# A feed-forward down projection by Strassen's seven products in eight of its eleven weight tiles, in a float32 kernel

## What is computed

```python
def swiglu(h, w_gate, w_up, w_down):
    return (jax.nn.silu(h @ w_gate) * (h @ w_up)) @ w_down
...
x = x + 0.5 * swiglu(rmsnorm(x, norm_g[layer, 0]), ffn_w_gate[layer, 0], ffn_w_up[layer, 0], ffn_w_down[layer, 0])
```

## Time and profile before

| | |
|---|---|
| median of 3 runs | 2626.75 us (2625.58 to 2626.8) |
| the profiled execution | 2626.32 us, of which the span is 2624.5 |
| granted TensorE clock, mean of the span | 0.999 |
| busy: TensorE, VectorE, ScalarE, GpSimd | 99%, 69%, 57%, 10% |
| HBM read over the span | 179 GB/s |

### The profile page before, as it was taken

How to read it: one execution, slowest core, us unless ns; L and a number is a source line. 1 busy time by engine, 2 the same in 40 slices (tenths; PEclk the granted TensorE clock), 3 DMA queues, 4 the chain that set the end, 5 groups by cost and what they waited for, 6 DMA issues and landing times.

```text
span 2624.5 us, 35122 instructions
## 1 busy us (share of the span) xinstructions
PE 2605.2 (99%) x14596; PEld 2241.7 (85%) x14596; DVE 1822.5 (69%) x2239; ACT 1493.7 (57%) x1974; POOL 258.6 (10%) x246
## 2 busy tenths in 40 slices
PE   8999999999999999999999999999999999999999
PEld 7888778888888878888889998888888899988888
DVE  6667766666667766666668887666666688876765
ACT  5456765445446655445457767454454577674543
POOL 0003210000004110000003123100000021231000
PEclk9999999999999999999999999999999999999999
DMA  7654445555555445555556464555555564645553
GB/s 239 198 189 161 161 158 182 191 193 182 189 175 181 152 161 188 189 184 193 192 166 187 138 211 159 179 190 190 179 193 193 167 189 135 210 159 183 186 193 128
DMA packets 342747, 471.84 MB, mean 180 GB/s; under 512 B 18810, under 2 KB 259516, under 8 KB 342588
## 3 DMA queue, kind: packets, MB, share of 16 engines
q1 hardware_dynamic: 342588, 469.61, 54.9%
HBM read 468.46 MB, written 1.11 MB: 179 GB/s over the span
## 4 chain that ended last, share of the span: by engine, by line
PE 94%; DVE 2%; ACT 2%; DMA 0%; issue 0%; SPq 0%; POOL 0%; DVEq 0%; ACTq 0%
PE PS L100 91%; PE PS L103 3%; DVE WL L109 1%; ACT ME L106 1%; ACT WH L106 1%; DMA ST<-in_ffn_w_gate 0%; DVE RL L117 0%; DVE XB L117 0%; DVE ME L109 0%; SPq L142 0%; ACT RH L106 0%; DVE SB L114 0%; POOL XB L109 0%; DVE SB L120 0%; DVE EA L109 0%
## 5 line engine op out<-in xcount | busy, mean ns | idle before, releaser
L109 DVE TENSOR_TENSOR WL<-ST,WH 128x2048 fp32r<-128x2048 f32 (+3 forms) x442 | 1005.5, 2275 | 352.8 <-ACT WH L106 351.7
L100 PE MATMUL PS<-XHL,WH 128*128 128x512 f32 (+1 forms) x4096 | 1123.6, 362 | 3.8 <-DVE GS L109 2.7
L106 ACT ACTIVATE WH<-ST 128x2048 fp32r<-128x2048 f32 (+3 forms) x442 | 830.7, 1880 | 144.4 <-PE PS L100 136.9
L100 PEld LDWEIGHTS PS<-XHL,WL 128*128 128x128 f32 x3456 | 652.8, 189 | 124.7
L100 PE MATMUL PS<-XHL,WL 128*128 128x256 f32 x3456 | 735.3, 279 | 0.0
L100 PEld LDWEIGHTS PS<-XHL,WH 128*128 128x128 f32 x4096 | 634.4, 190 | 12.9 <-DVE GS L109 2.8
L100 PE MATMUL PS<-WH,XHL 128*128 128x512 f32 (+3 forms) x1472 | 460.9, 387 | 0.0
L100 PE MATMUL PS<-WH,RH 128*128 128x512 f32 (+1 forms) x1056 | 410.3, 389 | 3.4 <-DVE RL L109 1.9
L100 PE MATMUL PS<-WL,RH 128*128 128x512 f32 (+1 forms) x1056 | 407.9, 386 | 0.0
L100 PE MATMUL PS<-WH,RL 128*128 128x512 f32 (+1 forms) x1056 | 407.6, 386 | 0.0
L100 PEld LDWEIGHTS PS<-WH,XHL 128*128 128x128 f32 x1472 | 273.7, 188 | 58.4 <-issue 7.3
(11 more groups left out here) (247 smaller groups left out, 1955.8 us busy)
## 6 DMA issues: line engine op xcount, KB each, us to landing
ST<-in_ffn_w SPq DMA_DIRECT2D x132, 1024.0 KB, 5.0
ST<-in_w_in SPq DMA_DIRECT2D x106, 1024.0 KB, 5.2
ST<-in_ffn_w_down SPq DMA_DIRECT2D x44, 1024.0 KB, 4.9
ST<-in_ffn_w_gate SPq DMA_DIRECT2D x43, 1024.0 KB, 5.3
ST<-in_ffn_w_up SPq DMA_DIRECT2D x43, 1024.0 KB, 5.3
ST<-in_w_ssd_out SPq DMA_DIRECT2D x16, 1024.0 KB, 5.0
ST<-in_w_branch SPq DMA_DIRECT2D x8, 1024.0 KB, 5.0
ST<-in_w_out SPq DMA_DIRECT2D x8, 1024.0 KB, 5.0
```

The source lines that it names most:

```text
L100: return self.eng.matmul(o, l, r, start=start, stop=stop) if self.eng else Said()
L106: return self.eng.activation(o, v, f, **kw) if self.eng else Said()
L109: return self.eng.tensor_tensor(o, a, b, op) if self.eng else Said()
```

## The change

Seen by blocks, a down tile is a 2 x 2 product: the hidden tile has four 128-column blocks (two k-halves by two halves of the 256 rows of X), the weight tile four 512-column blocks. Strassen's form (in Winograd's variant) has seven block products instead of eight, with sums of blocks on both sides.

- The phase's order becomes all 22 gate and up tiles (steps 0 to 21), then the eleven down tiles (steps 22 to 32). All eleven hidden tiles are kept.
- Down tiles 0, 5 and 10 (`PLAIN`) keep eight products. The other eight (`SUMMED`) take seven, four of them on sums of weight blocks (kind "t", in `TS`, split into `TH` and `TL`, rings of three) and three on the blocks themselves (kind "q", in `WH` and `WL`, of which the first 512 columns are no longer split for these tiles).
- `tile_sums` makes the weight sums on GpSimd, in float32 from `ST`, in three operations of 1024, 512 and 512 columns. `pair_sums` makes four sums of 128 columns of the hidden tile, and `scale_up` multiplies the up half by RBC, both on GpSimd. The reciprocal norm is now in the hidden tile, and no longer in the residual.
- `load_tile` waits for the sums of the tile that leaves its slot, besides its low part.
- All eight banks add up over the phase, one per kind of product (`MBANK`). Tiles 9 and 10 are run together, bank by bank. X is then put together from the eight banks and UM, by `add_um` (two SBUF inputs) and `add_product` (PSUM and X), one of the `add_um` on GpSimd.
- The transposes of X's first half follow the last bank's matmuls. The split of the next phase's first tile is made by GpSimd (`weights_lo` at the end of `pool_ffn`).
- The rope tables move to steps 16 to 18 of the first phase, and the transposes of the constants' gains from the first mixer's steps 0 and 1 to step 18 of the first phase.

```diff
-FFN = [("g", 0), ("u", 0), ("g", 1), ("u", 1)]
-for _i in range(2, NP):
-    FFN += [("g", _i), ("u", _i), ("d", _i - 2)]
-FFN += [("d", NP - 2), ("d", NP - 1)]
+FFN = [(_w, _i) for _i in range(NP) for _w in ("g", "u")] + [("d", _i) for _i in range(NP)]
 UP_AT = {i: FFN.index(("u", i)) for i in range(NP)}
 GATE_AT = {i: FFN.index(("g", i)) for i in range(NP)}
+DOWN = 2 * NP
...
+HIDDEN_AT = [max(UP_AT[i] + 1, 3) for i in range(NP - 1)] + [UP_AT[NP - 1] + 2]
...
+PLAIN = (0, 5, 10)
+SUMMED = [_i for _i in range(NP) if _i not in PLAIN]
+SEVEN = (("m1", 0, "q", 1), ("m2", 2, "q", 3), ("m3", 6, "q", 2), ("m6", 5, "t", 2), ("m5", 3, "t", 0), ("m7", 4, "t", 1),
+         ("m4", 1, "t", 3))
+EIGHT = (("m2", 1, "q", 1), ("m2", 3, "q", 3), ("m3", 1, "q", 0), ("m3", 3, "q", 2), ("c22", 0, "q", 0), ("c22", 2, "q", 2),
+         ("m4", 0, "q", 1), ("m4", 2, "q", 3))
+MBANK = {"m1": 0, "m6": 6, "m5": 4, "m7": 5, "m2": 1, "m3": 3, "c22": 7, "m4": 2}
...
+    def tensor_product(e, p, i, name, a, kind, c, begun, last=False):
+        tile, b = T0[p] + DOWN + i, MBANK[name]
+        c = slice(c * 512, (c + 1) * 512)
+        if kind == "q":
+            e.wait_ge(*at("lo", tile))
+            wh, wl = WH[:, tile % NR, c], WL[:, tile % NR, c]
+        else:
+            n = SUMMED.index(i) % 3
+            wh, wl = TH[n][:, c], TL[n][:, c]
+            e.wait_ge(*at("tl", p, i))
+        e.wait_ge(*at("hl", p, i))
+        first = b not in begun
+        if first:
+            clear(b)
+            begun.add(b)
+        fh, fl = HH[i][:, of(a)], HL[i][:, of(a)]
+        e.matmul(PS[:, b, :], fh, wh, first, False)
+        e.matmul(PS[:, b, :], fh, wl, False, False)
...
+                if i < NP - 2:
+                    for name, a, kind, c in EIGHT if i in PLAIN else SEVEN:
+                        m = tensor_product(e, p, i, name, a, kind, c, begun)
+                    m.then_inc(*e.done("tile", tile))
+                elif i == NP - 2:
+                    for group in MBANK:
+                        own = [(j, r) for j in (i, i + 1) for r in (EIGHT if j in PLAIN else SEVEN) if r[0] == group]
+                        for j, (name, a, kind, c) in own:
+                            m = tensor_product(e, p, j, name, a, kind, c, begun, (j, (name, a, kind, c)) == own[-1])
+                        m.then_inc(*e.done(group, p))
+                        if group == "m3":
+                            e.also("tile", tile)
+                    e.also("tile", tile + 1)
+                    freed.update({0: ("um", p), 1: ("x", p, 1, 1), 2: ("x", p, 0, 1), 3: ("x", p, 1, 0), 4: ("x5", p),
+                                  5: ("x7", p), 6: ("um", p), 7: ("x", p, 0, 0)})
+                    if p + 1 < len(phases):
+                        turn_x(e, p + 1, "", 0)
...
+        a, n = 512 if i in SUMS else 0, plan[i][0] * plan[i][1]
...
+    def sums_hi(e, p, i):
+        n = SUMMED.index(i)
+        e.wait_ge(*at("ts", p, i))
+        if n in (1, 2):
+            e.wait_ge(*at("tile", T0[p] + UP_AT[NP - 1]))
+        elif n > 2:
+            e.wait_ge(*at("tile", T0[p] + DOWN + SUMMED[n - 3]))
+        e.activation(TH[n % 3], TS[n % 3], ACT.Copy).then_inc(*e.done("th", p, i))
...
+            elif s == len(FFN) - 2:
+                e.wait_ge(*at("m1", p))
+                e.wait_ge(*at("tile", t0 + DOWN + NP - 3))
+                e.activation(UM, PS[:, MBANK["m1"], :], ACT.Copy, scale=0.5).then_inc(*e.done("uv", p))
+                weights_hi(e, t0 + s + 2)
...
+    def sums_lo(e, p, i):
+        e.wait_ge(*at("th", p, i))
+        n = SUMMED.index(i) % 3
+        e.tensor_tensor(TL[n], TS[n], TH[n].bitcast(F32), ALU.subtract).then_inc(*e.done("tl", p, i))
+    def hidden_lo(e, p, i):
+        e.wait_ge(*at("hh", p, i))
+        e.tensor_tensor(HL[i], H8[i][:, 128:128 + HN[i]], HH[i].bitcast(F32), ALU.subtract).then_inc(*e.done("hl", p, i))
+    def add_product(e, p, name, t, n, f, *done):
+        e.wait_ge(*at(name, p))
+        x = X[:, t, half(n)]
+        e.stt(x, PS[:, MBANK[name], :], f, x, ALU.mult, ALU.add).then_inc(*e.done(*done))
+    def add_um(e, p, t, n):
+        x = X[:, t, half(n)]
+        e.tensor_tensor(x, x, UM, ALU.add).then_inc(*e.done("xu", p, t, n))
...
+            if s == DOWN + NP - 3:
+                sums_lo(e, p, NP - 2)
+            if s < len(FFN) - 2:
+                weights_lo(e, t0 + s + 2)
+            if s + 1 - DOWN in SUMMED and s < DOWN + NP - 3:
+                sums_lo(e, p, s + 1 - DOWN)
...
+            if s == len(FFN) - 1:
+                e.wait_ge(*at("uv", p))
+                add_um(e, p, 1, 1)
+                e.wait_ge(*at("m6", p))
+                e.wait_ge(*e.last())
+                e.stt(UM, PS[:, MBANK["m6"], :], 0.5, UM, ALU.mult, ALU.add).then_inc(*e.done("um", p))
+                e.wait_ge(*e.last())
+                add_um(e, p, 1, 0)
+                add_um(e, p, 0, 0)
+                e.wait_ge(*at("xu", p, 1, 0))
+                add_product(e, p, "m5", 1, 0, -0.5, "x51", p)
+                e.wait_ge(*at("xu", p, 0, 0))
+                add_product(e, p, "m5", 0, 0, -0.5, "x5", p)
+                e.wait_ge(*e.last())
+                add_product(e, p, "m7", 0, 0, 0.5, "x70", p)
+                e.wait_ge(*at("xu", p, 1, 1))
+                add_product(e, p, "m2", 1, 1, 0.5, "x", p, 1, 1)
+                e.wait_ge(*at("x51", p))
+                add_product(e, p, "m3", 1, 0, 0.5, "x", p, 1, 0)
+                e.wait_ge(*at("xu", p, 0, 1))
+                add_product(e, p, "m7", 0, 1, 0.5, "x7", p)
+                e.wait_ge(*at("x70", p))
+                add_product(e, p, "c22", 0, 0, 0.5, "x", p, 0, 0)
+                if p + 1 < len(phases):
+                    split_x_lo(e, p + 1, "", 0)
+                e.wait_ge(*at("x7", p))
+                add_product(e, p, "m4", 0, 1, 0.5, "x", p, 0, 1)
+                weights_lo(e, t0 + s + 2)
...
+    def pool_ffn(e, p):
+        t0 = T0[p]
+        for s in range(len(FFN)):
+            for n, i in enumerate(SUMMED):
+                if s == DOWN - 3 + i + (n > 2):
+                    tile_sums(e, p, i)
+            for i in range(NP):
+                if s == UP_AT[i] + 1:
+                    scale_up(e, p, i)
+                if s == HIDDEN_AT[i] + 1 and i in SUMMED:
+                    pair_sums(e, p, i)
+        e.wait_ge(*at("um", p))
+        add_um(e, p, 0, 1)
+        weights_lo(e, t0 + len(FFN))
...
+    def scale_up(e, p, i):
+        h = HQ[i].rearrange("p (k t) -> p k t", k=2)
+        e.wait_ge(*at("us", p, i))
+        e.wait_ge(*at("rbc", p))
+        e.tensor_tensor(h, h, RBC[:, :].unsqueeze(1).to_broadcast([128, 2, T]), ALU.mult).then_inc(*e.done("un", p, i))
+    def pair_sums(e, p, i):
+        a21, a11, a22, a12, s1, s3, s2, s4 = (H8[i][:, of(j)] for j in range(8))
+        e.wait_ge(*at("m", p, i))
+        e.tensor_tensor(s1, a21, a22, ALU.add).then_inc(*e.done("s1", p, i))
+        e.tensor_tensor(s3, a11, a21, ALU.subtract).then_inc(*e.done())
+        e.wait_ge(*at("s1", p, i))
+        e.tensor_tensor(s2, s1, a11, ALU.subtract).then_inc(*e.done("s2", p, i))
+        e.wait_ge(*at("s2", p, i))
+        e.tensor_tensor(s4, a12, s2, ALU.subtract).then_inc(*e.done("s4", p, i))
+    def tile_sums(e, p, i):
+        tile, n = T0[p] + DOWN + i, SUMMED.index(i)
+        q = [ST[:, tile % NS, j * 512:(j + 1) * 512] for j in range(4)]
+        t1, t2, t4 = (TS[n % 3][:, j * 512:(j + 1) * 512] for j in (0, 2, 3))
+        e.wait_ge(*landed[tile])
+        if n > 2:
+            e.wait_ge(*at("tile", T0[p] + DOWN + SUMMED[n - 3]))
+        elif n == 2:
+            e.wait_ge(*at("m", p, NP - 2))
+        elif p == 0:
+            e.wait_ge(*at("gt", 3))
+            e.wait_ge(*at("cos", 1))
+            e.wait_ge(*at("rope_tables", 1))
+        e.tensor_tensor(TS[n % 3][:, 0:1024].rearrange("p (a c) -> p a c", a=2),
+                        ST[:, tile % NS, 512:1536].rearrange("p (a c) -> p a c", a=2),
+                        q[0].unsqueeze(1).to_broadcast([128, 2, 512]), ALU.subtract).then_inc(*e.done("t1", p, i))
+        e.wait_ge(*at("t1", p, i))
+        e.tensor_tensor(t2, q[2], t1, ALU.add).then_inc(*e.done("t2", p, i))
+        e.wait_ge(*at("t2", p, i))
+        e.tensor_tensor(t4, q[3], t2, ALU.subtract).then_inc(*e.done("ts", p, i))
...
+            if i - NS in SUMS:
+                e.wait_ge(*at("ts", *SUMS[i - NS]))
```

More of the change, by code:

```diff
@@ L541, in build @@
     NT = len(plan)
-    POOLED = set()
-    for p, (kind, l, j) in enumerate(phases):
-        POOLED |= {T0[p] + s for s in {"ffn": FFN_POOL, "mix1": MIX1_POOL, "mix2": MIX2_POOL}[kind]}
+    SUMS = {T0[p] + DOWN + i: (p, i) for p, (kind, _, _) in enumerate(phases) if kind == "ffn" for i in SUMMED}
     def view(W, i):
@@ L670, in r_row @@
         freed[b] = ("rbc", p)
+    def tensor_product(e, p, i, name, a, kind, c, begun, last=False):
[16 more added lines that the diff above has]
+        e.matmul(PS[:, b, :], fh, wl, False, False)
```

(51 more changed lines are left out.)

112 lines of the change are left out of this document (46 added, 66 removed).

## The result

The changed kernel took 2815.66 us (median of 4, 2812.4 to 2816.23) against 2626.16 of the kernel before measured beside it: ratio 1.0721, 95% interval 1.0702 to 1.0739. It is slower by 189 us; forecast were 2814 us, range 2735 to 2900.

The account below looks back on a forecast made before the run. TensorE, busy 99% of the span, was taken to bound the kernel before. Per phase 21.3 us (removed matmuls included) plus 2.2 at its end make 23.5, +188 in eight phases on 2626.3: 2814 us, range 2735 to 2900.

Parts of the forecast that it names:

- The gain: Eight summed down tiles a phase lose three matmuls of 0.2264 us each: 5.43 us a phase, 43.5 in eight phases.
- One at a time: Down stage: GpSimd's operations and VectorE's with two SBUF inputs exclude each other; a summed tile needs 8.25 us against TensorE's 4.75.
- The shared stretch: From step 20's start to the end of tile 9's sums: GpSimd 39.7, VectorE 36.7, handovers 1.4, about 78 us.
- Spans less 0.15, or whole spans: Each excluded operation overlaps the other engine's by about 0.15 us; the rival, exclusive for whole spans, gave 2879 us, chance 0.06.
- After the last sums: Rounding, split and signals 4.4 us, then matmuls and tile 10's split, up to the phase's last matmul: 14.2 us.
- the clock rival: TensorE's clock falls to 1.2 GHz in its waits; the last 45 matmuls take 10.2 us more a phase: 2896 us, chance 0.12.
- The phase's end: Transposes after the last matmul: X late by about 1.6 us, first low part 0.56 beyond the transposes, together 2.2 a phase.
- Costed at nothing: Gate and up stage, loads, SP queue, moved tables and gains, GpSimd's split of the next first tile: all hidden, 0 us.
- The signs named ahead: Profile after: TensorE about 91% busy, down-stage waits on sums' or weights' low parts, splits of 3 to 4 us, slower GpSimd additions.
- That they hardly exclude each other: Rival: GpSimd's and VectorE's down-stage work fits under TensorE, 2600 us, chance 0.09.
- Cheaper GpSimd operations: Rival: GpSimd's sums of a tile take 4.01 us instead of 4.96, total 2753 us and below, chance 0.09.
- Stalls in the in-order queues: Rival: ScalarE's 1.91 us rounding lies open for each summed tile, 15 us a phase more, around 2936 us, chance 0.06.

Follow-up runs that it names:

- the reduction: Changed kernel with VectorE's split of the weight sums replaced by a one-SBUF-input reduction of the same 2048 columns, low part left out: 2693.45 us.
- the five tiles on either engine: Changed kernel with five summed tiles (1, 3, 5, 7, 9) instead of eight: sums on VectorE 2621.08 us, sums on GpSimd 2684.37 us.
- the run with one tile: Changed kernel with only tile 9 summed, everything else of the change kept: 2637.82 us, ratio 1.0050 to the kernel before.
- four and five on GpSimd: Changed kernel with four summed tiles (2, 4, 6, 9) or five (1, 3, 5, 7, 9) instead of eight, sums on GpSimd: 2658.08 and 2684.37 us.
- the version that beats both: Changed kernel with five summed tiles, sums on VectorE, and X's first-half transposes ahead of m4's last three matmuls, c22 added earlier: 2615.97 us.
- filling the waits: Changed kernel plus repeats of product m3 in TensorE's waits for the sums: 2825.47 us with twelve matmuls more a tile, 2812.24 with nine.

## Why the prediction was right

The mechanism was right. That the time (2814 against 2815.66) is so near is partly luck: two terms missed in opposite directions, and the phases took 22.3 to 26.8 us more where 23.5 was forecast for each. Held against the phase from 442 us:

- **The gain.** Three matmuls a summed tile go, as said. Their worth was taken as 0.2264 each; in the new order the down matmuls at full clock start 0.232 apart, where they started 0.227 apart. The prediction had no such term. Where TensorE is the bound, as with one or five tiles, that eats 1.3 us a phase; here only the last group's part of it (0.2 us) lies on the path.
- **One at a time.** The shared stretch, from step 20's start (551.78, two tiles of 5.57 us ahead of the first down matmul at 562.92) to the last sums' end (627.91 + 1.31 = 629.22), took 77.4 us; the sum was 78. The mechanism is shown by the reduction (122 us less for an operation of equal length that reads one SBUF tile); the five tiles on either engine (63 us) agree with it.
- **Spans less 0.15, or whole spans.** By whole spans the stretch would be 86 us. 77.4 agrees with the overlap seen in the earlier trace rows. That rival is out. The Trainium skill (SBUF — State Buffer, Who interferes with whom) calls the shared port pair an exclusive lock; its words on the whole instruction stand at VectorE's 2-port modes, and the prediction read them for two SBUF inputs too. The same section of the Trainium skill says that a VectorE instruction with at most one SBUF input, outside those modes, does not contend with GpSimd; the reduction's 2286 ns agree.
- **After the last sums** the sum had 14.2 us, and it took 17.0 (to the transposes at 646.21). Of the 2.8 over, 2.7 are 14 matmuls at 0.427 us at the start of the last group: the clock rival came true in part. The sum gave that term nothing; the rival had all 45 matmuls at the lower level, 10.2 us. TensorE had waited 2.0 us, worked 3.7 and waited 3.1 before it; the granted clock of 633.5 to 646.2 was 0.76. Five phases have such a slow start of the last group; in the three others it had none.
- **The phase's end** was put at 2.2 us and took 1.2 (0.82 until the next phase's first matmul beyond the transposes, where the sum had 0.56, and 0.37 at the second half, where it had nothing). The 1.6 us that the sum had for X being late didn't come: X was in time, as TensorE itself came later, and in the three phases with a fast last group it was 0.4 late. In the run with one tile the end cost the same 1.2.
- **Costed at nothing.** Gate and up tiles kept their pace; loads, the SP queue and GpSimd's split of the next first tile (5.09 us) show no wait of TensorE. That held. The moved tables did cost one wait, at step 18 of the first phase, where they keep VectorE from emptying banks that TensorE needs:

```profile
117.66 0.73 PE L111 MATMUL PS<-XHL,WH 128*128 128x512 f32 x2 [1.64 <-DVE GS L120]
```

- **The signs named ahead.** Waits on TL in the down stage only (and 13.7 us on bank 7, which weren't named), splits of 2.75 and 3.15 to 3.3 us where 3 to 4 were named, GpSimd's additions far over 2.40 and 1.28: as forecast. TensorE is busy 94%, not 91%, about half of it since slow matmuls count as busy.
- **Rivals.** That they hardly exclude each other is refuted by the rows of VectorE and GpSimd above and by the reduction. Cheaper GpSimd operations: alone they cost what the earlier trace rows say. Stalls in the in-order queues didn't matter at eight tiles; they did at four and five on GpSimd, where my own forecasts were too low by 37 and 14 us.

## What to carry to other kernels

An idle engine isn't free help when it shares a way into memory with a busy one: before work is moved from VectorE to GpSimd, add up for both all operations with two SBUF inputs and compare the sum, not the larger of the two, with the bound; one engine may do both shares in less time. A saving of 1/8 of the matmuls needs every engine that feeds them to have that much to spare at that place, not over the run: 69% busy over the span was no room in a stage that asked VectorE for 4 us and GpSimd for 5 in each 4.75. And a latency chain (landing, sums, rounding, split) needs its own check once the totals fit.

## What was unexpected of the hardware

- The down matmuls' spacing rose from 0.227 to 0.232 us with the new order and buffers, with nothing else at work on TensorE, also in the version that beats both. Moving the stationary high parts by 32 or 96 bytes didn't bring it back, but raised it by 1 ns more. Open.
- Waits of TensorE between stretches of work were enough for the granted clock to fall to its lower level (1.2 GHz) for 22 to 31 matmuls in a down stage. In every phase it fell after the longest wait, of 5.1 us; in the phase from 1071 us it fell once more at 1257.6, where no wait since 1230 had been longer than 2.0 us. Most of the slow matmuls lay where TensorE had to wait anyway: filling the waits took 211 of them down to 76 and won 5.7 us.
- With GpSimd and VectorE both busy all the time, each waits for one operation of the other in turn: splits of 1.75 us took 2.75 on average, additions of 1.28 took 2.5. Neither starves.
